# Attention C: side work between outputs and transpositions, its parts one step sooner, a gate projection one part later

## The reference

```python
q = (rmsnorm_2(cq, g_cq) @ w_cq_b).reshape(B, S, H_C, C_NOPE + C_ROPE)
kv = (rmsnorm_2(ckv, g_ckv) @ w_ckv_b).reshape(B, S, H_C, C_NOPE + C_V)
k_nope, v_c = kv[..., :C_NOPE], kv[..., C_NOPE:]
qc = rmsnorm_2(q, gq_c)
kc = rmsnorm_2(jnp.concatenate([k_nope, k_pe], -1), gk_c)
...
oc = attend_blocks(qc, kc, v_c, (C_NOPE + C_ROPE) ** -0.5)
...
o = jnp.concatenate([oc.reshape(B, S, -1), od.reshape(B, S, -1)], -1) * jax.nn.silu(gate)
```

## Time and profile before

| what | value |
|---|---|
| median of 3 runs | 3858.34 us (3854.77 to 3859.18) |
| profiled execution, its own time | 3851.71 us |
| its span | 3849.7 us |
| PE busy | 96% of the span |
| DVE, ACT, POOL busy | 51%, 34%, 27% |
| mean granted clock of PE | 0.987 |
| attention C (first score to last output) | 2999 to 3391 us |

### The profile page before, as it was taken

How to read it: one execution, slowest core, us unless ns; L and a number is a source line. 1 busy time by engine, 2 the same in 40 slices (tenths; PEclk the granted TensorE clock), 3 DMA queues, 4 the chain that set the end, 5 groups by cost and what they waited for, 6 DMA issues and landing times.

```text
span 3849.7 us, 51842 instructions
## 1 busy us (share of the span) xinstructions
PE 3699.4 (96%) x21561; PEld 2906.7 (76%) x21561; DVE 1981.7 (51%) x2505; ACT 1326.0 (34%) x1603; POOL 1023.6 (27%) x634
## 2 busy tenths in 40 slices
PE   8999999999999999999999999999999999999988
PEld 7778888878788887888888777666677566767767
DVE  8464455524652537333413556655743655456663
ACT  3343433322330112111201344455624666444440
POOL 4212222222233345666433311110022001111001
PEclk9999999999999999999999999999999999999999
DMA  4111111111125422222522211100121001111011
GB/s 147 34 53 47 49 50 45 50 44 47 55 80 183 148 88 66 82 82 83 202 82 73 79 44 48 39 17 9 53 72 48 14 13 27 31 26 25 17 57 67
DMA packets 283160, 238.56 MB, mean 62 GB/s; under 512 B 16976, under 2 KB 255728, under 8 KB 282928
## 3 DMA queue, kind: packets, MB, share of 16 engines
q1 hardware_dynamic: 262128, 166.04, 14.8%
q10 hardware_dynamic: 20800, 69.22, 5.1%
HBM read 181.81 MB, written 49.35 MB: 60 GB/s over the span
## 4 chain that ended last, share of the span: by engine, by line
PE 82%; DVE 10%; ACT 4%; issue 2%; POOL 0%; DMA 0%; ACTq 0%; SPq 0%; DVEq 0%; POOLq 0%
PE ps L401 19%; PE ps L418 18%; PE ps L451 15%; PE ps L902 9%; DVE AR L2474 3%; PE ps L1273 2%; DVE SM L3306 2%; PE ps L701 2%; DVE AR L2482 2%; PE ps L1284 1%; PE ps L1264 1%; PE ps L1295 1%; PE ps L348 1%; PE ps L503 1%; PE ps L1344 1%
## 5 line engine op out<-in xcount | busy, mean ns | idle before, releaser
L3439 POOL CAST WH<-WR 128x1024 fp32r<-128x1024 f32 (+2 forms) x231 | 242.8, 1051 | 2567.5 <-DMA WR<-in_w_in 820.8
L3441 POOL TENSOR_TENSOR WL<-WR,WH 128x1024 fp32r<-128x1024 f32 (+2 forms) x231 | 500.9, 2169 | 18.5
L2474 DVE TENSOR_TENSOR AR<-AR 128x512 f32<-128x512 f32 (+3 forms) x426 | 452.0, 1061 | 56.5 <-ACT AR L1822 38.1
L418 PE MATMUL ps<-ARR,WH 128*128 128x512 f32 x1472 | 366.0, 390 | 2.2 <-ACT ARR L1919 2.2
L418 PEld LDWEIGHTS ps<-ARR,WH 128*128 128x128 f32 x1472 | 277.1, 188 | 60.5 <-ACT ARR L1919 2.7
L401 PE MATMUL ps<-XH,WH 128*128 128x512 f32 (+2 forms) x1168 | 300.2, 400 | 3.9 <-DVE AR L2474 1.7
L401 PE MATMUL ps<-XH,WL 128*128 128x512 f32 (+2 forms) x1168 | 290.1, 391 | 0.0
L401 PE MATMUL ps<-XL,WH 128*128 128x512 f32 (+2 forms) x1168 | 288.7, 389 | 0.0
L401 PEld LDWEIGHTS ps<-XH,WH 128*128 128x128 f32 (+2 forms) x1168 | 216.4, 188 | 57.2 <-issue 7.1
L3306 DVE TENSOR_REDUCE SM<-ps 128x1 f32<-128x1024 f32 x128 | 156.7, 1224 | 194.6 <-PE ps L1273 113.5
L401 PEld LDWEIGHTS ps<-XH,WL 128*128 128x128 f32 (+2 forms) x1168 | 218.3, 187 | 49.0
(11 more groups left out here) (295 smaller groups left out, 6255.8 us busy)
## 6 DMA issues: line engine op xcount, KB each, us to landing
WR<-in_w_in SPq DMA_DIRECT2D x78, 512.0 KB, 3.8
gates<-AR ACTq DMA_DIRECT2D x54, 512.0 KB, 2.7
AR<-gates SPq DMA_DIRECT2D x54, 512.0 KB, 4.4
H<-spill ACTq DMA_DIRECT2D x32, 512.0 KB, 6.1
WR<-in_w_in_e SPq DMA_DIRECT2D x26, 512.0 KB, 3.8
spill<-H ACTq DMA_DIRECT2D x24, 512.0 KB, 2.7
WR<-in_w_ffn_in SPq DMA_DIRECT2D x24, 512.0 KB, 3.8
WR<-in_w_in_o SPq DMA_DIRECT2D x23, 512.0 KB, 3.8
```

What stands on the lines that cost most here:

```text
L418: mm = pe.matmul(pt[:, h * 512:h * 512 + 512], wp[:, w % 4, k, :], xp(k)[:, h * 512:h * 512 + 512], start=i == 0, stop=i == 3 * nk - 1)
L2474: return v.tensor_tensor(o, x, y, op)
L3439: pool.tensor_copy(hi, full).then_inc(s_whi, 1)
L3441: pool.tensor_tensor(lo, full, hi, ALU.subtract).then_inc(s_wsplit, 1)
```

## The change

On TensorE the side part now stands between the outputs and the transpositions of a step instead of behind the transpositions. On all three engines the first part runs ahead of the loop (`next(side)`), so that part k runs in step k-1 instead of step k. In heads 4 and 6 the gate projection `gc` moves from part 1, ahead of `kc`, to part 2, behind `hn`, on TensorE and on ScalarE. The order of ScalarE and VectorE within a step stays: their part stands at the end of the step.

```diff
                 hq(("qc", h), "w96", 96)
+                gemm(("kc", h), cols(wckv, h * 128, 64, nk=1), rhs=lambda k: A(28), m=64, nk=1)
+                yield
+                pe.wait_ge(s_kraw, h - 1)
+                hn(("kc", h), "w96", [A(22)], 96)
                 if h % 2 == 0 and p >= 2:
                     xgemm(("gc", p), cols(wio, OG + p * P))
-                gemm(("kc", h), cols(wckv, h * 128, 64, nk=1), rhs=lambda k: A(28), m=64, nk=1)
-                yield
-                pe.wait_ge(s_kraw, h - 1)
-                hn(("kc", h), "w96", [A(22)], 96)
                 yield
...
                         mm.then_inc(filled[n % 4], 1)
+                    if kind == "C":
+                        yield
                     if 1 <= s < nu + 1:
...
                             mm.then_inc(filled[n % 4], 1)
-                    yield
+                    if kind == "B":
+                        yield
...
-            weave(att_c(), itertools.chain(chain(4, *[prep_c(h) for h in range(2, 8)]), chain(8, prep_d(0))))
+            side = itertools.chain(chain(4, *[prep_c(h) for h in range(2, 8)]), chain(8, prep_d(0)))
+            next(side)
+            weave(att_c(), side)
...
                 qroot()
-                if h % 2 == 0 and p >= 2:
-                    last = ("O", BASE["C"] + 8 * (p - 2) + 7)
-                    act.wait_ge(freed[bank(last)], turn(last))
-                    gate(("gc", p), A(14 + p % 2))
                 act.wait_ge(filled[bank(("kc", h))], turn(("kc", h)))
...
                 root()
+                if h % 2 == 0 and p >= 2:
+                    last = ("O", BASE["C"] + 8 * (p - 2) + 7)
+                    act.wait_ge(freed[bank(last)], turn(last))
+                    gate(("gc", p), A(14 + p % 2))
                 yield
```

More of the change, by code:

```diff
@@ L1127, in prep_c @@
                 hq(("qc", h), "w96", 96)
-                if h % 2 == 0 and p >= 2:
-                    xgemm(("gc", p), cols(wio, OG + p * P))
                 gemm(("kc", h), cols(wckv, h * 128, 64, nk=1), rhs=lambda k: A(28), m=64, nk=1)
@@ L1133, in prep_c @@
                 hn(("kc", h), "w96", [A(22)], 96)
+                if h % 2 == 0 and p >= 2:
+                    xgemm(("gc", p), cols(wio, OG + p * P))
                 yield
```

## The result

The changed kernel takes 3918.79 us in the median of four runs (3915.44 to 3927.64), the kernel before 3858.76 (3854.77 to 3864.49). The ratio is 1.0158 with a 95% interval of 1.0136 to 1.018: slower by 1.6%, where 1.1% was forecast, and inside the range.

The account below looks back on a forecast made before the run. TensorE, busy 96% of the span, was taken as the bound. New waits of 53.6 us, less 15.8 saved, plus 6 for clock gave +43.8 us on 3858.3: 3902 us, range 3880 to 3922.

Parts of the forecast that it names:

- (a): Query projection `qc` alone (heads 4, 6, `qd`): second score waits 1.85 us for its tile, three times, 5.6 us.
- (b): `vct` and `qc` (heads 3, 5, 7): first score waits 2.47 us, second 0.43; three times, 8.7 us.
- (c): `hq` and key projection (heads 3 to 7, and D): scores wait 2.4 us, six times, 14.4 us.
- (e): Single-copy side jobs (`vc` three times, `vd`, `vdt`): scores wait 0.7 us, five times, 3.6 us.
- (f): Gate projection `gd`: a score waits for ScalarE's table load and pass, 2.0 us.
- (h): Head 2, at the start: `hn` waits for ScalarE's four key passes, then later waits follow; 0 to 5.5, taken as 4 us.
- (d): Key sums `hn`, alone, with `gc` behind (heads 4, 6) or in D's part: scores wait, 10.3 us in all.
- (g): Behind six query sums, VectorE's root and rotation delay the next exponential: 0 to 1.4 us each, 5 us in all.
- first case: Attention C: side work's tiles hold up the next scores, +24 to +64 us; chance 0.74.
- (second): Same tile waits in attention C, but half absorbed as other engines catch up: +10 to +24 us; chance 0.10.
- (third): Every new TensorE wait, some 24 of 0.7 us and more, costs clock: +76, 3934 us; chance 0.08.
- (fourth): Old waits ahead of transpositions and new pairs go, with tiles free in time: 3839 us; chance 0.05.

Follow-up runs that it names:

- e3: Kernel before with side work between outputs and transpositions on TensorE and the gate projection one part later, but no part a step sooner: 3923.82 us.
- e4: Kernel before with only the gate projections of heads 4 and 6 one part later: 3851.52 us, ratio 0.9989.
- e2: Changed kernel with TensorE's side work back behind the transpositions, keeping parts one step sooner and the gate later: 3847.31 us.
- e1: Changed kernel with ScalarE's side part ahead of its copies of the transposed probabilities in attention C: 3858.99 us.
- e7: Changed kernel with ScalarE's second copy of the transposed probabilities done twice in attention C: 3969.0 us.
- e6: Changed kernel with the second copy of the transposed probabilities on VectorE instead of ScalarE in attention C: 3911.48 us.
- e5: Changed kernel with ScalarE's side part ahead of the copies of the transposed probabilities in steps of part 0 only: 3909.82 us.

## Why the prediction was right, and what it had too small

- **The tile order as the cause** held in every test: e3 has it, with only the gate's move beside it, which costs nothing in e4, and loses 68 us of stage; e2 lacks it and loses nothing; e1 keeps TensorE's order and takes nearly all of the loss away by ScalarE's order alone; e7 lengthens it; and in e6 the waits follow the copy to the engine that now has it.
- **The sum of waits** was 53.6 us and measured 51.9; less 15.8, +36.1 where +37.8 was said. By terms: (a) 6.5 for 5.6, (b) 7.5 for 8.7, (c) 13.3 for 14.4 (five times 2.21, once 2.24), (e) 3.6 for 3.6, (f) 2.0 for 2.0, (h) 3.8 for 4. (d) was too large, 6.2 for 10.3: in D's part and in head 7 the wait came ahead of T instead. (g) was too small, 9.0 for 5: two waits ahead of T were 3.4 and 3.5 us, which the last section takes up. That the sum came so near is in part luck, since the misses of (d) and (g) cancel. The waits ahead of new pairs are gone, as said.
- **The clock was mis-sized**, and this is the step that was too small. It took 9 us for drops, little over five at 1.7 us, less 3.0: +6. Measured: 25.7 us more busy time. Both factors were short. The profile of the changed kernel has eleven drops: ten behind its fifteen waits of 2.0 us and more (twelve had been counted), and one at the start of the stage behind a wait of 0.97, which e2, e3 and e4 have too, so that it is hardly the change's own. And a drop cost (25.7 + 3.0) / 11 = 2.6 us on average: of the windows of 7 us behind the eleven, six have a clock of 0.76 as in the earlier trace rows, the others 0.51 to 0.63. Nor was much of a drop covered: the waits came at nearly their full sum beside it.
- **The range** held the result in part by luck. Its first case was to reach from (g), (h) and the clock at 0 to these at their upper ends, +24 to +64. Worked out from the terms, that is 53.6 - 5 - 4 - 15.8 - 3.0 = +25.8 to 53.6 + 3.4 + 1.5 - 15.8 + 20 - 3.0 = +59.7. The medians differ by 60.0, at that end, since (g) and the clock both came out above what they were given at most.

Two scores behind the same wait, and one behind a longer one, show the price. TensorE, changed kernel, in heads 3, 4 and 6:

```profile
3065.25 3.90 PE L1273 MATMUL ps<-AR 96*128 96x512 f32 x8 [2.21 <-DVE AR L2489]
...
3110.27 5.40 PE L1273 MATMUL ps<-AR 96*128 96x512 f32 x8 [2.21 <-DVE AR L2489]
...
3246.18 5.72 PE L1273 MATMUL ps<-AR 96*128 96x512 f32 x8 [2.52 <-DVE AR L2489]
3251.83 3.43 PE L1284 MATMUL ps<-AR 128*64 128x128 f32 x32
```

The windows of 7 us behind these three waits:

```profile
3110.27:3117.27 7.00, 7.00 (x38) 3.63 (x40) 6.72 (x9) 5.04 (x5) 0.00 (x0) 0.76 0.00 0
3065.25:3072.25 7.00, 6.67 (x56) 3.96 (x56) 6.73 (x9) 5.03 (x5) 0.00 (x0) 1.00 0.01 2
3246.18:3253.18 7.00, 7.00 (x22) 3.20 (x24) 5.86 (x5) 4.45 (x5) 3.10 (x2) 0.63 0.00 0
```

At 1.00 the eight score matmuls take 3.90 us with their end; with the clock at half for a part of them or longer they take 5.40 or 5.72, and at 3246 the outputs, 1.97 elsewhere, are slow as well (3.43): the drop at 3110 costs 7 x 0.24 = 1.7 us, that at 3246 costs 7 x 0.37 = 2.6. The prediction had priced all drops by the one at the earlier trace rows.

The direction was that of the Trainium skill's section on cycling through PSUM banks ("TensorE: Matmul & The Clock Gate", "A second HAM failure mode: psum-queue depth-cycling"): short waits between groups, clock swinging between two levels. The trace agrees as to the long ones: 0.94 over the stage instead of 0.99. As to waits of 1.85 us and less it does not: behind them the changed kernel's clock stayed at 1.00, but for the one at the start of the stage.

The rivals: that standing lets the others catch up (second) does not show, since (a) to (c) came to 27.3 us of 28.7. That each new wait costs clock (third) fails: there were eleven drops, not 24, and 3918.8 us instead of 3934. Faster (fourth) is out; its first condition, ScalarE emptying the side work's tiles ahead of the copies of T, is what e1 made, and there the outputs wait instead: 3859, not 3839. Gain against loss is out too.

## What to carry to other kernels

Where jobs take buffers in turn, moving work in one engine's order changes who inherits which buffer. Ask for each job who had its buffer four jobs ago, and whether the engine that empties it has something else first; an engine that is half idle still delays, because it works in order. Where producers are reordered, reorder the emptying too, or leave both, and price each wait of over 2 us on TensorE with the clock that it may take along.

## What the runs showed of the hardware

**Clock behind short waits.** Over the nine profiles of attention C I took each wait of TensorE with the clock at full level ahead of it, and the mean clock of the 7 us that follow. It was under 0.95 behind 4 of 49 waits of 1.2 to 1.6 us, 5 of 20 of 1.6 to 2.0, 13 of 25 of 2.0 to 2.4, 19 of 21 of 2.4 to 2.8 and 21 of 22 longer ones. Shorter waits are not free of it: the one drop of the kernel before stands behind a wait of 0.70 us and one of 0.26. So equal waits fall on both sides, as the two of 2.21 us above, and e5 lost waits but little of the clock. What decides among equal ones was not tried.

**VectorE slowed beside GpSimd.** The wait of 3.4 us ahead of T in head 7 has the place of one of 0.67 in head 3. The query's root on VectorE in head 7, then two of its lines in head 3 (columns as in the earlier trace rows):

```profile
3290.08 1.07 DVE L2489 SCALAR_TENSOR_TENSOR AR<-AR 128x16 f32<-128x16 f32 x2
3291.19 2.21 DVE L2485 TENSOR_SCALAR AR<-AR 128x16 f32<-128x16 f32 x1
3293.44 3.72 DVE L2481 TENSOR_TENSOR AR<-AR 32x1024 f32<-32x1024 f32 x3
...
3065.23 0.39 DVE L2489 SCALAR_TENSOR_TENSOR AR<-AR 128x16 f32<-128x16 f32 x2
3065.65 0.18 DVE L2485 TENSOR_SCALAR AR<-AR 128x16 f32<-128x16 f32 x1
```

And GpSimd at the time of the first three, where it splits a weight tile:

```profile
3289.89 1.04 POOL L3448 CAST WH<-WR 128x1024 fp32r<-128x1024 f32 x1 [11.77 <-DMA WR<-in_w_in_o]
3291.00 2.37 POOL L3450 TENSOR_TENSOR WL<-WR,WH 128x1024 fp32r<-128x1024 f32 x1
```

A scaling of 16 columns that takes 0.18 us in head 3 takes 2.21 here, and ends at 3293.40, when GpSimd's subtraction ends at 3293.37. With the two passes ahead of it VectorE loses 2.71 us; the scores' maximum, the exponential and T come later by it, and the wait of T is 2.72 us longer. The Trainium skill ("SBUF — State Buffer", "Who interferes with whom") says that VectorE and GpSimd share a pair of ports, which some of VectorE's instructions need beside its own, among them those with two inputs in SBUF and a TENSOR_SCALAR that runs in a two-port mode, and that the engine which issues first holds the pair for its whole instruction while the other stands. The two ends, 0.03 us apart, fit that.

The wait of 3.5 us in D's part is of the same kind: there GpSimd's subtraction runs from 3359.65 to 3362.01, and the three passes of VectorE's rotation, begun at 3359.84, take 5.77 us. In e7 the subtraction there ends at 3403.98, ahead of the scaling at 3404.25; the scaling takes 0.17 us, the rotation 3.74, and T does not wait. No run was made to move the split alone, so the cause is read from such rows and not shown by a change of its own.
